# One core of Trainium2: decays ahead of the next weight split on ScalarE, and transposed probabilities, their product with V and a maximum at other places among the matmuls

## The reference, cut to what matters

```python
xn = rms_norm(x, g_mix)
z = xn @ w_in                                   # q | k | v | forget logits | lru x | lru gate
att = forgetting_attention(q, [past_k, k], [past_v, v], [past_logf, logf], n_past)
xc = causal_conv(xl, state_conv, w_conv, b_conv)
r, i = sigmoid(xc @ w_a + b_a), sigmoid(xc @ w_x + b_x)      # per block of 128
a = exp(-8 * r * softplus(-lambda))
h_t = a_t * h_{t-1} + sqrt(1 - a_t**2) * (i_t * xc_t)
x = x + concat(rms_norm(att), rms_norm(gelu(gl) * h)) @ w_out
x = x + relu(rms_norm(x) @ w_up)**2 @ w_down
```

## Time and profile before

| | |
|---|---|
| median of 3 runs | 2304.42 us (2301.89 to 2305.88) |
| the profiled execution | 2305.47 us, its span 2303.9 us |
| PE busy | 2252.2 us, 98% of the span |
| DVE busy | 1605.5 us, 70% |
| ACT busy | 858.1 us, 37% |
| chain that ended last | PE 86%, DVE 7%, issue 2%, DVEq 2% |
| PE waits that the profile names | L2096 for DVE's PR: 12.0 us in 7 times; all others 5.9 us or less |

### The profile page before, as it was taken

One profiled execution on the slowest core, in us unless ns is written; L12 is line 12 of the kernel. 1 busy time (PEld: TensorE's weight loads), 2 busy tenths in 40 slices (PEclk: granted clock), 3 DMA queues, 4 the chain that ended last, 5 costly groups with the idle time before them and its releaser, 6 DMA issues.

```text
span 2303.9 us, 50021 instructions
## 1 busy us (share of the span) xinstructions
PE 2252.2 (98%) x19889; PEld 2202.1 (96%) x19889; DVE 1605.5 (70%) x2043; ACT 858.1 (37%) x1201; POOL 154.6 (7%) x194
## 2 busy tenths in 40 slices
PE   7999999999999999999999999999999999999997
PEld 7999898989988999999999999999999999999997
DVE  7349889888884697876576576576576576576563
ACT  5124433434354333343343243243243243243245
POOL 0001111111104031000000000000000000000002
PEclk8999999999999999999999999999999999999998
DMA  7457999999985243333433433433433433433422
GB/s 238 106 159 260 323 327 329 305 311 327 319 285 185 97 135 88 108 103 102 128 101 100 129 98 100 131 97 100 132 95 100 134 94 100 136 92 100 137 87 98
DMA packets 386972, 368.47 MB, mean 160 GB/s; under 512 B 12259, under 2 KB 350596, under 8 KB 385844
## 3 DMA queue, kind: packets, MB, share of 16 engines
q1 hardware_dynamic: 359828, 295.38, 41.7%
q0 software_dynamic: 18608, 67.64, 8.2%
q10 hardware_dynamic: 8448, 4.20, 0.6%
HBM read 354.22 MB, written 12.94 MB: 159 GB/s over the span
## 4 chain that ended last, share of the span: by engine, by line
PE 86%; DVE 7%; DVEq 2%; issue 2%; ACT 1%; DMA 1%; ACTq 0%; SPq 0%
PE PS L1897 36%; PE PS L1901 18%; PE PS L2343 9%; PE PS L2342 9%; PE PS L2341 9%; DVE KR L1350 2%; PE PS L2058 2%; DVEq L1508 1%; DVE SC L1352 1%; PE PS L2106 1%; DVE WL L1214 1%; PE PS L2248 1%; PE PS L2096 0%; ACT WH L744 0%; DVE NM L1507 0%
## 5 line engine op out<-in xcount | busy, mean ns | idle before, releaser
L1094 ACT ACTIVATE WH<-RAW 128x1024 fp32r<-128x1024 f32 x293 | 304.7, 1056 | 680.9 <-PE PS L1901 521.5
L1648 DVE TENSOR_TENSOR WL<-RAW,WH 128x1024 fp32r<-128x1024 f32 x293 | 358.3, 1223 | 133.7 <-ACT WH L1094 131.8
L1897 PE MATMUL PS<-XH,WH 128*128 128x260 f32 x1952 | 407.0, 290 | 10.8 <-DVE XL L1279 5.9
L1897 PE MATMUL PS<-HH,WH 128*128 128x260 f32 x2048 | 412.4, 282 | 1.4 <-DVE HL L1653 0.7
L1901 PE MATMUL PS<-HH,WL 128*128 128x260 f32 x2048 | 411.7, 282 | 0.0
L1897 PE MATMUL PS<-HL,WH 128*128 128x260 f32 x2048 | 410.8, 282 | 0.0
L1901 PE MATMUL PS<-XH,WL 128*128 128x260 f32 x1952 | 394.8, 284 | 0.0
L1897 PE MATMUL PS<-XL,WH 128*128 128x260 f32 x1952 | 394.6, 284 | 0.0
L1751 DVE TENSOR_TENSOR A<-A,PS 128x520 f32<-128x520 f32 x256 | 177.4, 696 | 264.3 <-PE PS L1901 263.5
L1897 PEld LDWEIGHTS PS<-XH,WH 128*128 128x128 f32 x1952 | 303.0, 190 | 22.6 <-issue 13.3
L1897 PEld LDWEIGHTS PS<-HH,WH 128*128 128x128 f32 x2048 | 314.6, 188 | 2.1 <-issue 1.1
(11 more groups left out here) (335 smaller groups left out, 3087.5 us busy)
## 6 DMA issues: line engine op xcount, KB each, us to landing
KR<-in_cache_k POOLq DMA_DIRECT2D x128, 512.0 KB, 6.0
VR<-in_cache_v SPq DMA_DIRECT2D x128, 512.0 KB, 6.3
RAW<-in_w_up SPq DMA_DIRECT2D x128, 512.0 KB, 4.2
RAW<-in_w_down SPq DMA_DIRECT2D x128, 512.0 KB, 4.4
RAW<-in_w_in SPq DMA_DIRECT2D x82, 512.0 KB, 8.4
RAW<-in_w_out SPq DMA_DIRECT2D x32, 512.0 KB, 5.3
TMP<-in_w_up SPq DMA_DIRECT2D x30, 512.0 KB, 6.2
xT_spill<-A SPq DMA_DIRECT2D x1, 4160.0 KB, 16.5
```

Of the source, the lines that this page charges most:

```text
L1094: nc.scalar.activation(RING_H[SLOT[i]], RB[b], ACT.Copy).then_inc(f_hi, 1)
L1648: V.tensor_tensor(RING_L[SLOT[i]], RB[op_block(i)], RING_H[SLOT[i]].bitcast(F32), ALU.subtract).then_inc(f_lo, 1)
L1897: mm(dsts[c], wh(k), x[:, k, c * HT:(c + 1) * HT], start=first and n == 0 and x is xh, stop=False)
```

## The change

Three things move; nothing is added or taken away. On ScalarE `gates` makes tanh and exp right after the sigmoids and only then the high part of the next weights (`next_hi`), and the broadcast query QB is copied after the square root, not ahead of it. On TensorE `max_all` goes from half product 25 of unit 0 to 21, `transpose_probs` from (2,7) to (2,15), and `attend` from (2,19) to (2,27). The tail behind the loop (the last head) has its own places and keeps them, but uses the same `gates`.

```diff
-            def gates(h, after_sigmoids, between):
+            def gates(h, next_hi, broadcast_query):
...
                 nc.scalar.activation(PR[:, T + SEQ:2 * T], PS[:, 6, NB:2 * NB], ACT.Sigmoid, bias=bx).then_inc(sig_done, 1)
-                after_sigmoids()
                 act.wait_ge(sig_done, h + 1)
                 nc.scalar.activation(PT[:, 0:T], PR[:, 0:T], ACT.Tanh, scale=CPOS[:, one(h)])
                 nc.scalar.activation(PR[:, 0:T], PR[:, 0:T], ACT.Exp, scale=CNEG[:, one(h)]).then_inc(decay_done, 1)
-                between()
+                next_hi()
 
                 act.wait_ge(ratio_ready, h + 1)
                 nc.scalar.activation(PT[:, 0:T], PT[:, 0:T], ACT.Sqrt).then_inc(root_done, 1)
+                broadcast_query()
...
-                    extra[0, 25] = lambda: max_all(i)
+                    extra[0, 21] = lambda: max_all(i)
                     extra[1, 5] = head_scores
-                    extra[2, 7] = lambda: transpose_probs(i - 1)
-                    extra[2, 19] = lambda: attend(i - 1)
+                    extra[2, 15] = lambda: transpose_probs(i - 1)
+                    extra[2, 27] = lambda: attend(i - 1)
```

## The result

The changed kernel takes 2287.31 us (median of 4 runs, 2286.29 to 2287.92) against 2304.9 for the kernel before, timed beside it. The ratio is 0.9928, 95% interval 0.9914 to 0.9941: faster by 17.6 us. The profiled execution took 2287.92, its span 2286.3 against 2303.9.

What follows compares the result with a forecast made beforehand. The loop was taken to be bound by a chain through several engines, seen as TensorE's wait at the transposes: 7 waits, 12.0 us, plus 0.1 in the tail, 12.1 in all, giving 2292.3 us, range 2289 to 2299.

Steps and rivals of the forecast that it cites:

- What bounds the kernel: Loop step: a chain through several engines sets 67.47 us; TensorE's only wait there is 1.74, before the transposes.
- rival one: Loop steps: transfers set the pace, so a step stays at 67.47 us and the time at 2304; chance 0.05.
- rival two: Loop steps: key pages under a busier VectorE give back 5.6 us in seven steps, time 2297.9; chance 0.12.
- The hold-up of GpSimd's transfers: Key pages: VectorE's copies could delay their issue, 16.8 us in seven steps, 2309; not in the trace, moves no chance.
- rival three: Value pages at (2,21): a landing of 16.7 us would lose 7 us in seven steps, 2311; chance 0.03.
- What it gives back is exactly that wait: Transposes eight half products later: only the 1.74 us wait goes, 12.0 us in 7 times.
- TensorE's own 65.73 us: Loop step: with the wait gone, TensorE's busy time of 65.73 us is the new pace.
- In time this is worth nothing further ... it is insurance: Earlier maximum: margin at the transposes grows from 1.2 to about 2.6 us, no time unless VectorE is delayed over 1.2.
- Is there a slower cycle?: Loop step: old chain 63.1 us, VectorE without its two waits 63.1, so TensorE is the slowest.
- Were it left at its place ... the earlier decays would have been for nothing: Maximum left at its old place: VectorE would stand until 480.86 as before, so the earlier decays win nothing.
- The smaller steps: Within a step: tanh and exp 1.62 us earlier, high part in time, maximum 1.44 earlier, VectorE's waits 1.5 and near 1.0.
- the tail: Behind the loop: the last head keeps its places; ScalarE's new order shortens the XL wait of 2.1 us by 0.1.

Runs made afterwards that it cites:

- later_only: The kernel before with only the transposes and the product with V eight half products later; 2292.73 us, ratio 0.9952.
- later_and_max: The kernel before with all three new places on TensorE (transposes, product with V, maximum) but ScalarE's old order; 2288.1 us, ratio 0.9927.
- after_rows13: The changed kernel with the transpose of the maxima moved from (0,15) to directly behind the query product at (0,13); 2287.39 us, ratio 0.9927.
- after_max25: The changed kernel with the maximum back at (0,25); 2293.46 us, ratio 0.9956.
- after_apart: The changed kernel with the transposes of v two slices behind those of k, not directly behind them; 2288.11 us, ratio 0.9933.

## Why the prediction was right in its direction and wrong in its size

**What bounds the kernel: right.** The only repeated wait of the loop sat in front of L2096. With it gone the whole change wins 17.6 us, and *later_only*, which takes away nothing else, 11.1 of the row's 12.0. A transfer ceiling (rival one) isn't there: a step now moves 331 GB/s as worked out. VectorE's waits for key pages are 1.8 us in 4 in the whole span, short of one margin, so rival two didn't come. The hold-up of GpSimd's transfers by a copy of VectorE that the Trainium skill tells of ("SBUF — State Buffer", SBUF: two separate sides) isn't seen in the changed kernel either: its 128 issues of key pages take 527 to 562 ns. The value pages at (2,21) brought no wait (rival three).

**"What it gives back is exactly that wait": mis-sized.** This is the term of 12.0. A stop costs 1.96 us a step, 0.22 above its named 1.74. The end of TensorE's last pair before a stop, 0.17 us, and 0.05 of slower transposes behind it are booked as busy, so the list of waits doesn't have them. In i = 1 the stop cost more, since the clock had fallen behind it in the profile before: 1.6 us, which the prediction had no row for: its windows are of later steps, at a clock of 1.00. Whether an execution has the fall is chance, as far as these runs show.

**"TensorE's own 65.73 us": wrong.** That number was its busy time *with* the stop in it. Without the stop and with the maximum at its old place it is 65.50, with the maximum at the value pages 65.14.

**"In time this is worth nothing further ... it is insurance": the step that failed.** The maximum's move is worth 5 to 6 us (2293.46 with all but it, 2287.31 with it; 2292.73 against 2288.1 with ScalarE's old order). The step counted only the chain into the transposes, and two things were left out. One is the ring by SELQ and the query product, which comes next once the stop is gone: 66.1 to 66.5 us with the maximum at (0,25). Behind the value pages the maximum stands 1.65 us earlier in the step (14.27 us behind the gates before, 12.62 now), so the ring is about 64.5 to 64.9, just below TensorE's 65.14. "Is there a slower cycle?" was asked, and VectorE's cycle was priced "without its two waits" at 63.1. But VectorE can't go round without the maximum, which it gets from TensorE; with that way in it the ring was about 66.0, more than the 65.73 that was taken for the new pace. No wait named it, since TensorE's stop had TensorE come 1.49 us after the column was ready. The other is the place itself, 0.36 us a step.

**The account of 17.6 us.** Seven stops of 1.96, less the 0.4 by which the last step was shorter (67.06 for 67.46), make 13.3; the maximum's place 0.36 in six steps 2.2 (in i = 1 no value pages stand ahead of it); the clock in i = 1 1.6; the ends 0.5. That is 17.6, between the two profiled executions; the medians differ by as much. Of these the ring takes nothing, since the whole change keeps it below TensorE; it takes its share only where the maximum is left behind. There *later_only* came near the forecast of 12.1 by the luck of two errors that cancel: its steps win 13.3 + 1.6 and lose 3.0 to the ring (what its steps i = 3 to 7 are above 65.50). Its trace has 12.1 us in the seven steps and 1.4 at the ends; by the medians it is 11.1, so 2.4 us lie between one profiled execution and the medians, part of which can be the clock in i = 1.

**"Were it left at its place ... the earlier decays would have been for nothing": right, and more than that.** Decays alone gave 0.9995, and with everything else in place they add nothing either (2288.1 without, 2287.31 with, equal steps). With ScalarE's old order VectorE reaches the maximum at 479.87, so its move can bring only the wait of 0.98. The ring is then at 65.1 to 65.3 (an estimate, from the 66.1 to 66.3 of *later_only*), about TensorE's pace, and one step of *later_and_max* was 65.69. The new order may thus be the insurance here, but that isn't shown: *after_rows13*, which has it, also had one long step, 65.75.

**The smaller steps.** L1369's wait was forecast at 1.5 and is 1.13; L1423's at 1.0 and is 0.89; tanh comes 0.13 behind the sigmoids and not 0.05. The maximum came 1.65 us earlier in the step and not 1.44. Exp stands ahead of the high part, which is in time. Of these only the maximum's hour bears on the time; the others are right within 0.4 us and set nothing. For the tail 0.1 us was forecast; the XL wait went from 2.1 to 2.0.

## What to carry to other kernels

When the one repeated wait of a loop goes, the loop falls to the next ring, and that may have no row in the list of waits, because the old wait covered it. Walk the rings before pricing: from each instruction that one engine waits for on the other, through that engine's whole step, back to its own. The trace gives an estimate of a ring's length: the step, less the time by which the handed-over piece was ready before it was asked for (here 67.47 - 1.49 = 66.0, and 66.1 to 66.5 came). Compare each length with the new pace, and treat a move that shortens one as a term and not as insurance. And don't take the busy time of a loop that stops for its pace without the stop: here 65.73 was 65.50, and 65.14 with the maximum at its new place.

## What the runs showed of the hardware

- A stop of TensorE costs more than its idle time in the trace, by 0.22 us whether it is long or short: 1.96 us for 1.74 (*before* against *later_only*), 0.80 for 0.58 (*after_max25*), 0.59 for 0.37 (*later_only*).
- Behind the same stop of 1.84 to 1.86 us in i = 1 the clock was at 0.50 for 3.4 us in 4 of 6 profiles, 1.6 us of time; one stop of 1.48 there and the stops of 1.74 in the later steps had no fall behind them. Why the one and not the other is open.
- A slice of 128x260 matmuls behind the 64 small ones of the value pages or behind the 8-row one takes 0.35 us to its second pair and not 0.24; the maximum costs 0.29 us more one slice behind the pages and 0.36 two behind them, while the 0 to 0.04 and 0.00 of *after_rows13* and *after_apart* show that this is no cost of every small piece. What in the machine makes it wasn't settled.
